# Turning the attention weights on VectorE with a DRAM bounce, in a two-layer trunk on one core

## The reference

```python
def memory_attention(q, mem_k, mem_v):            # 4 heads of 128, 256 memory tokens
    s = jnp.einsum('bthd,bmhd->bhtm', qh, kh) * (MEM_HEAD_DIM ** -0.5)
    p = jax.nn.softmax(s, axis=-1)
    o = jnp.einsum('bhtm,bmhd->bthd', p, vh)

def stick_breaking_attention(q, k, v):            # 12 heads of 128, causal
    mask = key_pos[None, :] < q_pos[:, None]
    z = jnp.einsum('bhqd,bhkd->bhqk', q_blk, kh) * scale
    log_beta = jax.nn.log_sigmoid(z)
    log_keep = jnp.where(mask, jax.nn.log_sigmoid(-z), 0.0)
    later = lax.cumsum(log_keep, axis=3, reverse=True) - log_keep
    w = jnp.where(mask, jnp.exp(log_beta + later), 0.0)
    o = jnp.einsum('bhqk,bhkd->bhqd', w, vh)
```

## Time and profile before

| | before |
|---|---|
| time, median of 3 runs | 1468.18 us |
| span of the profiled execution | 1466.5 us |
| TensorE busy | 1458.0 us, 99% |
| VectorE, ScalarE busy | 68%, 49% |
| chain that ended last | 99% TensorE |
| mean busy share of the DMA engines, 933 to 1248 us | about 0.8 |

### The profile page before, as it was taken

The page is one execution under the profiler, slowest core; times in us unless marked ns, Lnnn a source line. Parts: engine busy times, 40 slices in busy tenths (PEclk is TensorE's granted clock), DMA queues, the critical chain, the costliest instruction groups (busy, mean ns, idle before and its releaser), DMA issues.

```text
span 1466.5 us, 18207 instructions
## 1 busy us (share of the span) xinstructions
PE 1458.0 (99%) x6842; PEld 1221.7 (83%) x6842; DVE 997.5 (68%) x1317; ACT 716.3 (49%) x1066; POOL 122.8 (8%) x184
## 2 busy tenths in 40 slices
PE   9999999999999999999999999999999999999998
PEld 7888888888888888888888888888888888888886
DVE  6775568465576896856579676556566566578987
ACT  6764544444544645763325654433333433455465
POOL 0001111111110000000010001111111011000000
PEclk9999999999999999999999999999999999999999
DMA  9877788777886987477989876687888888858853
GB/s 344 290 287 225 159 215 228 174 235 158 212 251 165 323 323 260 155 262 282 358 326 372 291 224 219 244 218 196 230 241 244 202 239 208 226 188 329 315 200 144
DMA packets 154189, 357.97 MB, mean 244 GB/s; under 512 B 7824, under 2 KB 23440, under 8 KB 150032
## 3 DMA queue, kind: packets, MB, share of 16 engines
q1 hardware_dynamic: 103824, 205.98, 40.3%
q0 software_dynamic: 29376, 102.77, 28.3%
q10 hardware_dynamic: 20928, 48.41, 9.0%
HBM read 310.99 MB, written 113.25 MB: 289 GB/s over the span
## 4 chain that ended last, share of the span: by engine, by line
PE 99%; DMA 0%; SPq 0%; ACT 0%; issue 0%; DVE 0%; ACTq 0%
PE main L2128 25%; PE main L2127 25%; PE main L2126 25%; PE aux L2127 6%; PE aux L2126 6%; PE aux L2128 6%; PE aux L2484 2%; PE aux L2473 1%; DMA w_raw<-in_w_mem_kv 0%; PE aux L2270 0%; PE main L2178 0%; PE aux L2178 0%; PE main L2199 0%; PE main L2202 0%; PE main L2205 0%; PE aux L2220 0%
## 5 line engine op out<-in xcount | busy, mean ns | idle before, releaser
L2126 PE MATMUL main<-act_hi,w_hi 128*128 128x512 f32 x1216 | 475.3, 391 | 0.0
L2127 PE MATMUL main<-act_lo,w_hi 128*128 128x512 f32 x1216 | 473.6, 389 | 0.0
L2128 PE MATMUL main<-act_hi,w_lo 128*128 128x512 f32 x1216 | 473.6, 389 | 0.0
L2128 PEld LDWEIGHTS main<-act_hi,w_lo 128*128 128x128 f32 x1216 | 228.3, 188 | 47.4
L2127 PEld LDWEIGHTS main<-act_lo,w_hi 128*128 128x128 f32 x1216 | 228.4, 188 | 46.7
L2126 PEld LDWEIGHTS main<-act_hi,w_hi 128*128 128x128 f32 x1216 | 228.4, 188 | 46.4
L1334 DVE SCALAR_TENSOR_TENSOR w_lo<-w_raw,gains,w_hi 128x512 fp32r<-128x512 f32 x180 | 123.3, 746 | 120.5 <-ACT w_hi L704 120.5
L704 ACT ACTIVATE w_hi<-w_raw,gains 128x512 fp32r<-128x512 f32 x180 | 115.4, 712 | 140.6 <-PE main L2128 121.9
L1325 DVE TENSOR_TENSOR w_lo<-w_raw,w_hi 128x1024 fp32r<-128x1024 f32 x88 | 104.1, 1222 | 105.2 <-ACT w_hi L697 105.0
L697 ACT ACTIVATE w_hi<-w_raw 128x1024 fp32r<-128x1024 f32 x88 | 88.5, 1057 | 169.5 <-PE main L2128 132.7
L2126 PE MATMUL main<-w_hi,act_hi 128*128 128x512 f32 (+1 forms) x432 | 163.5, 378 | 0.0
(11 more groups left out here) (321 smaller groups left out, 1861.4 us busy)
## 6 DMA issues: line engine op xcount, KB each, us to landing
w_raw<-in_w_in_a SPq DMA_DIRECT2D x32, 1024.0 KB, 6.7
w_raw<-in_w_in_b SPq DMA_DIRECT2D x32, 1024.0 KB, 7.9
weight_sums<-in_w_out_a POOLq DMA_DIRECT2D x48, 512.0 KB, 7.0
weight_sums<-in_w_out_b POOLq DMA_DIRECT2D x48, 512.0 KB, 7.2
weight_sums<-weight_sums POOLq DMA_DIRECT2D x32, 512.0 KB, 6.4
w_raw<-weight_sums SPq DMA_DIRECT2D x16, 1024.0 KB, 6.6
work<-weight_sums SPq DMA_DIRECT2D x16, 1024.0 KB, 7.5
w_raw<-in_w_mem_kv SPq DMA_DIRECT2D x13, 1024.0 KB, 5.2
```

Of the source, the lines that this page charges most:

```text
L2126: TE.matmul(o, a[0], b[0], start=first, stop=False)
L2127: TE.matmul(o, a[0], b[1], start=False, stop=False)
L2128: return TE.matmul(o, a[1], b[0], start=False, stop=final)
```

## The change

TensorE's transposes are gone in both attentions. For each head, VectorE turns the weights in blocks of 32x32 (`V.transpose`) and lays them out so that a DMA can put the blocks of the four partition quarters in their places: ScalarE's queue stores 128 rows to DRAM (`turn_scratch`, 5 KB a row, or `prob_scratch`, 4 KB a row), waits for the store, and loads them back in four DMAs of 32 partitions, each row in four pieces of 1280 or 1024 bytes. The loads land in `wt_lo` or `pmt_lo`. ScalarE then copies the high part from there and VectorE subtracts in place. The values read the turned blocks with a strided pattern. The loads of keys and values move to SP's queue, between slab loads, each behind a wait for the values of the head two before. The heads' steps are laid out by slot; scores of head 1 are in slot 1, before head 0's values in slot 2, and so on. POOL's weight sums count on one semaphore, and each of the four groups waits for the group before.

```diff
@@ ScalarE @@
+            def turn_store(i, h):
+                act.wait_ge(wt_turned, 4 * (4 * i + h) + 4)
+                act.dma_start(turn_dram.rearrange("r i c m -> (r i) (c m)"), turned).then_inc(turn_stored, 16)
+
+            def turn_load(i, h):
+                n = 4 * i + h
+                act.wait_ge(turn_stored, 16 * (4 + n) + 16)
+                if h:
+                    act.wait_ge(o_done, n)
+                for c in range(4):
+                    act.dma_start(wt_lo[32 * c:32 * c + 32, :].rearrange("p (r m) -> p r m", r=4).bitcast(F32),
+                                  turn_dram[:, :, c, :].rearrange("r i m -> i r m")).then_inc(turn_loaded, 16)
+
+            def turned_high(i, h):
+                n = 4 * i + h
+                act.wait_ge(turn_loaded, 64 * (4 + n) + 64)
+                for b, w in enumerate(WT_WIDTH):
+                    part = slice(512 * b, 512 * b + w)
+                    nc.scalar.activation(wt_hi[:, part], wt_lo[:, part].bitcast(F32), ACT.Copy).then_inc(wt_high, 1)
...
                         split_next(G, j)
+                        if slot == 0:
+                            stick_weights(i, 0)
+                        if slot == 1:
+                            turn_store(i, 0)
+                            turn_load(i, 0)
+                            turned_high(i, 0)
+                            stick_weights(i, 1)
+                        if slot == 2:
+                            turn_store(i, 1)
+                            turn_load(i, 1)
+                        if slot == 3:
+                            turned_high(i, 1)
+                            stick_weights(i, 2)
+                        if slot == 4:
+                            turn_store(i, 2)
                             gate_sigmoid(2 * i + (G_B + 1))
+                            turn_load(i, 2)
+                            turned_high(i, 2)
+                        if slot == 5:
+                            stick_weights(i, 3)
+                            turn_store(i, 3)
+                        if slot == 6:
+                            turn_load(i, 3)
+                            turned_high(i, 3)
@@ ScalarE, memory head j @@
                         mem_head(L, j + 1)
+                    probs_store(L, j)
...
                     if j == 3:
                         act.wait_ge(sum_ready, 6 * L + 1)
                         y_quad(q_k1[0], 1)
+                    probs_load(L, j)
                 mem_probs_out(L, 3)
@@ VectorE, at the end of stick_weights @@
+                dve.wait_ge(w_ready, 4 * n + 4)
+                for k in range(NT):
+                    V.transpose(*turn_blocks(k)).then_inc(wt_turned, 1)
@@ VectorE, slots @@
+                        if slot == 5:
+                            turned_low(i, 2)
                         split_next(G, j)
...
                         if slot == 3:
+                            turned_low(i, 1)
                             dve.wait_ge(y_stored, 16 * i + 64)
                             dve.wait_ge(v_stored[3], 64)
                             gate_out(G, 0)
                             gate_out(G, 1)
+                            stick_weights(i, 2)
+                            gate_out(G, 2)
+                            gate_out(G, 3)
@@ VectorE, end of mem_norm_probs @@
+                dve.wait_ge(p_ready, 4 * L + n + 1)
+                V.transpose(pm_turned.rearrange("p (c n j) -> p n c j", c=4, j=32),
+                            pm.rearrange("p t (m c i) -> p (t m) c i", m=NMB, i=32)).then_inc(pt_turned, 1)
@@ SP @@
+            def load_kv(n):
+
+                if n > 1:
+                    sp.wait_ge(o_done, n - 1)
+                if n < 3:
+                    sp.wait_ge(v_stored[min(n + 1, 3)], 64)
+                sp.dma_start(kv[:, n % 2, :, :].bitcast(F32), kv_dram[n]).then_inc(kv_loaded[n % 2], 16)
@@ TensorE, hooks @@
+                        if slot == 0:
+                            hooks = {1: lambda: stick_scores(i, 0)}
+                        if slot == 1:
+                            hooks = {3: lambda: stick_scores(i, 1)}
+                        if slot == 2:
+                            hooks = {1: lambda: stick_values(i, 0)}
+                        if slot == 3:
+                            hooks = {2: lambda: stick_scores(i, 2), 3: lambda: stick_values(i, 1)}
+                        if slot == 5:
+                            hooks = {0: lambda: stick_scores(i, 3), 2: lambda: stick_values(i, 2)}
+                        if slot == 7:
+                            hooks = {0: lambda: stick_values(i, 3)}
@@ TensorE, memory attention and the projection behind it @@
-                    hooks = {(1 if j == 0 else 0): lambda: mem_scores(L, j), 3: lambda: mem_transposed(L, j)}
+                    hooks = {(1 if j == 0 else 0): lambda: mem_scores(L, j)}
...
-                half(s, 0, m01, 0, 0, values)
-                half(s, 1, m01, 0, 1)
+                half(s, 0, m01, 0, 0, freed(0))
+                half(s, 1, m01, 0, 1, values)
```

More of the change, by code:

```diff
@@ L63 @@
 WT_WIDTH = (512, 512, 256)
+TURN_AT = (0, 4, 7, 9)
+KV_LOADS = {8 * i + at: 4 * i + h for i in range(NPAIR) for at, h in ((7, 1), (10, 2), (11, 3), (13, 4))
+            if 4 * i + h < NB}
+PROB_TURN = (0, 16)
 Z_ORDER = ((1, 3, 0), (0, 2, 384), (2, 2, 0), (3, 1, 0))
@@ L222, in trunk, with probs_back @@
         pmt_lo = split_at("pmt_lo", [P, NMB, T], 2, 1024)
+        pm_turned = work[:, 1024:2048]
+        pmt_at = [w[:].rearrange("p m t -> p (m t)") for w in (pmt_hi, pmt_lo)]
+        def probs_back(w, m):
+            return w.rearrange("p (r t m j) -> p m t r j", r=4, t=NT, m=NMB)[:, m]
         mo = four(3)
@@ L430, in trunk @@
         q22_loaded = [sem(f"q22_loaded{n}") for n in range(2)]
-        sums_made = [sem(f"sums_made{n}") for n in range(4)]
+        sums_made = sem("sums_made")
         sum_ready = sem("sum_ready")
@@ L474, in load_in @@
                         sp.dma_start(x_nat[:, 2 + j, :], x_v[:, 2 + j, :]).then_inc(nat_loaded[1], 16)
+                if G0 == G_B:
+                    for q in range(1, 2 * NPAIR + 2):
+                        for j in range(4):
+                            n = KV_LOADS.get(4 * q + j)
+                            if n:
+                                load_kv(n)
+                            load_slab(G0 + q, j, w[:, in_column(q):in_column(q) + C])
+                    return
                 with sp.Fori(0, NPAIR - 1) as i:
@@ L2268, in mem_transposed @@
                 for m in range(NMB):
[L2269 to L2276 removed]
                     last = three_passes(aux[:, 2, :], (mv_hi[:, n % 2, m, :], mv_lo[:, n % 2, m, :]),
[L2278 removed]
+                                        [probs_back(w, m) for w in pmt_at], m == 0, m == NMB - 1)
                 last.then_inc(mo_done, 1)
@@ L2464, in stick_scores @@
                                  (kv[:, h % 2, 0, 0:w], kv[:, h % 2, 1, 0:w])).then_inc(z_done, 1)
-            def stick_transposed(i, h):
-                pe.wait_ge(w_ready, 4 * (4 * i + h) + 4)
-                for k in range(NT):
-                    bank, at = ((1, 0), (2, 0), (3, 0), (2, 384))[k]
-                    for t in range(k, NT):
-                        o = aux[:, bank, at + P * (t - k):at + P * (t - k) + P]
-                        c = T - P * (t + 1) + P * k
-                        last = TE.transpose(o, beta[:, t, c:c + P], ident[:])
-                last.then_inc(wt_done, 1)
             def stick_values(i, h):
```

216 lines of the change are left out of this document (112 added, 104 removed).

## The result

The changed kernel takes 1588.88 us (median of 4 runs, 1587.55 to 1589.55) against 1468.68 us of the kernel before on the same chip (4 runs, 1468.07 to 1469.37). The ratio is 1.0818, with a 95% interval of 1.0802 to 1.0833: 120 us slower. The forecast was 1492 us, its range ended at 1525. The sign and the mechanism were right; one term of the sum, the length of a trip in the loop, was 16.4 us where 11.0 stood, and the lower clock, which stood among the rivals, came on top.

The account below looks back on a forecast made before the run. TensorE was taken as the bound, busy 1458.0 of 1466.5 us. With the transposes' saving counted, the loop gave +9.9 and the memory attentions +14.4: +24.3 us, 1490.8 profiled, median 1492; 8-in-10 range 1447 to 1525.

Parts of the forecast that it names:

- The saving: TensorE's transposes removed: 13.1 us for 12 loop heads and 7.0 us for 8 memory heads, 20.1 us on the path.
- Turning on VectorE: VectorE's block transposes: 1.75 us for a loop head's four turns of 1280 columns; 1.2 us for a memory head.
- The chain, 66.2 + 4R: Loop turn length with four trips in sequence, R each; 110.2 us at R = 11.0, against 106.9 before.
- R in the loop: Loop trip, from last VectorE transpose to landing of the fourth load: 11.0 us, range 7.4 to 13.
- 5.5 a leg: Loop trip's store and its four loads, each put at 5.5 us by scaling the 7.2 us of 1 MB loads.
- the loop's term: Loop's part of the sum: a turn 3.3 us longer than before, three turns +9.9 us.
- Rival 3: Trips fall in step with GpSimd's bursts: trip 13 us in the loop, 11.8 in memory attentions; 1528 us, chance 0.12.
- 28.1 + 4R': Memory attention: time from slab 0's start to the last landing, four trips of R' each; +7.2 us per attention.
- R': Memory attention trip of 512 KB: 10.0 us for three heads, 8.5 for the last; break-even 7.8.
- Rival 4: TensorE's clock falls in gaps, a quarter slab at half speed after each of nine: 24 us more, 1516, chance 0.12.
- Key and value loads "hidden": Loop's key and value loads on SP's queue, with a slab load behind: wanted 22 us later against 8.5, so no cost.
- rivals 2 and 3: The first: in-between trips, 9.5 us in loop, 8.6 in memory attentions; 1465 us, chance 0.09. The second: see Rival 3.

Follow-up runs that it names:

- experiment 2: Changed kernel with each DMA of GpSimd's weight sums moving one row of 256 and the output projections reading input weights: 1507.1 us.
- experiment 3: Changed kernel with the loop's five trip DMAs moving an eighth of their bytes, high and low parts made from the turned blocks in place: 1544.6 us.
- experiment 4: Changed kernel with the loop's store cut into four DMAs of 1280-byte pieces and the load made one DMA: 1567.6 us.
- experiment 1: Changed kernel without both trips to DRAM, high and low parts made from the turned blocks in place: 1452.9 us, ratio 0.9893 to the kernel before.
- the filling: Changed kernel with matmuls without use in two gaps of each memory attention, loop untouched: 1582.4 us, ratio 1.0778 to the kernel before.
- experiment 5: Changed kernel with the loop's key and value loads moved from SP's queue to ScalarE's, behind the turned loads: 1590.5 us.

## Why the prediction was wrong, by its own steps

- **The saving**, 20.1 us, was right: without trips 1452.9, the turn 102.6.
- **Turning on VectorE**: 1024 columns take 1.25 us (1.2 put), four turns of a head 1.69 (1.75 put). Right.

```profile
426.64 1.25 DVE L1618 STREAM_TRANSPOSE work<-work 128x1024 f32<-128x1024 f32 x1
...
1051.65 1.69 DVE L2071 STREAM_TRANSPOSE work<-work 128x512 f32<-128x512 f32 x4
```

- **The chain, 66.2 + 4R**, was right in each of its parts. On ScalarE's and TensorE's timelines, second and third turn (us):

| part | forecast | experiment 2 | changed |
|---|---|---|---|
| values 3 to the next turn's first store | 28.2 | 28.3, 28.3 | 31.0, 30.3 |
| landing 0 to store 1 | 10.75 | 10.7 | 10.7 |
| landing 1 to store 2 | 12.0 | 11.9 | 11.9 |
| landing 2 to store 3 | 13.0 | 13.3 | 13.3 |
| landing 3 to values 3 | 2.25 | 2.4 | 2.4 |
| the turn's own four trips | 44.0 | 44.5, 43.9 | 61.9, 67.1 |

  What differs in the changed kernel besides the trips is the first line, the one in which the chain runs over TensorE's own work. That 131.8 came so near 131.2 has some luck in it: with the turn's own trips the formula gives 128.1 and 133.3, and the clock makes up the rest. Experiment 3's 120 us are 112 by the formula, 2.9 of clock, 3.9 of late keys and values, and 0.9 for the wait that its edit adds.
- **The step that failed is R in the loop.** "5.5 a leg": the store leg is that, 5.2. The load leg is 11.3, twice its term, and the ceiling of 13 for the trip lies at the least of the twelve. Three things were wrong in it. I scaled the 7.2 us of a 1 MB load down by its bytes, but experiment 3 shows that only a quarter of a trip goes with the bytes, and even those 7.2 became 11.1 with the trips beside them (median of the loop's ten). I took four DMAs as one with "three more issues"; the cut costs 1.7 to 3.5 us (experiment 4), and the issues are 0.31 to 2.16 us each. And I didn't ask what the new order issues beside the loads: SP's slab load behind VectorE's split (experiment 2). Twelve trips of 5.4 us more are 65 of the 73 us that the loop's term lacks; most of the rest is the clock, below.
- **Rival 3**, the step with GpSimd's bursts, was the right one, and too mild: it put the burst at 2 us a trip; experiment 2 shows 5.3. Its place is the load leg (11.3 to 8.1) more than the store's (5.2 to 3.0).
- **The memory attentions**: the second one bore out 28.1 + 4R'. Its trips are 11.5, 10.2, 9.6 and 7.5 us where I had 10, 10, 10 and 8.5; the last landing should come 66.9 us after slab 0's start and comes at 68.2. In the first the trips are 18.0, 14.0, 10.4 and 7.6: 78.0 by the formula, 79.1 measured. So R' was right for one stage and I gave it to both; in the first, GpSimd's sums are issued until 464.50, and with their bytes away (experiment 2) its trips are 12.3, 10.2, 9.4 and 7.6. These are the second stage's waits; the first values wait most, and the half slab behind the last values waits as well:

```profile
1381.27 0.77 PE L2245 MATMUL aux<-pmt_hi,mv_hi 128*128 128x512 f32 x1 [6.47 <-DVE pmt_lo L1625]
1398.22 0.48 PE L2245 MATMUL aux<-pmt_hi,mv_hi 128*128 128x512 f32 x1 [0.71 <-issue]
1425.56 0.47 PE L2245 MATMUL aux<-pmt_hi,mv_hi 128*128 128x512 f32 x1 [0.63 <-issue]
```

  They and the 3.46 us of the half slab are 11.3 us; I had put 10.7. Some 5 us I had not counted at all: with the same matmuls TensorE is busy 4.9 us longer than in experiment 1 from the first scores to the end (5.8 in the first memory attention's stretch), which is the lower clock.
- **Rival 4**, the clock: it does fall in the gaps, as the Trainium skill has it (TensorE: Matmul & The Clock Gate, Why this matters for your kernels). A turn of the changed kernel, in the columns of the row in experiment 1:

```profile
1073.09:1204.26 131.17, 109.99 (x480) 0.90 0.83 232
```

  TensorE is busy 110.0 us with work that takes 102.6 at full clock. Most of that costs nothing, since the chain of trips sets the turn and TensorE's waits are only shorter. But from values 3 to the next scores the chain runs over TensorE, and there the lower clock is paid. The changed kernel, then experiment 2, from values 3 to the next store:

```profile
1204.26 3.89 PE aux L2586 x12
...
1234.54 6.61 DMA turn_scratch<-work
```

```profile
1151.53 2.18 PE aux L2587 x12
...
1179.85 2.90 DMA turn_scratch<-work
```

  From values 3 to the next scores it is 18.3, 17.6 and 18.1 us against 15.7 each time: 6.9 us in the loop. With the 3 us that the filling gave back in the memory attentions, some 10 of the 37 us are shown on the path: less than the 24 of my rival, and not in my sum at all.
- **Key and value loads "hidden"**: not by name, 18.6 us of waits, for loads that take 14.4 us where I had 7.2. They hang behind values that are late themselves, and in the changed kernel each lands before the trip that VectorE waits for (experiment 5); with the shorter trips of experiment 3 one of them does cost.
- **Slips in the working.** 5.4 less 0.8 plus 1.2 is 5.8, not 5.6 (measured: 5.7 to 6.9 from a landing to the next store in the memory attentions). With 8.5 for the last trip the memory terms of rivals 2 and 3 are +3.0 and +12.6, not +2.5 and +13.3. None of them changes the outcome.

## What to carry to other kernels

The time of a small DMA beside heavy traffic is not its bytes' share of a large one's: count what it waits for, once for each DMA that must land, and take the issues with it. Look also at which loads the new order lets go at the same moment. Before a trip to DRAM replaces work on the busy engine, write down the chain with the trip as a letter; the formula with its break-even (here 10.2 us) was right when the number put into it was not, and it says what to try: not a shorter trip but one that runs beside the next step. And a clock that falls in a gap costs only where the engine is the one that the rest waits for; find that stretch on the chain and price it there.

## What the runs showed of the hardware

- GpSimd's transfers of 512 KB, which hold 42% of the DMA engines' time in the loop, add 5.3 us to a store and load pair of 640 KB on ScalarE's queue (11.1 to 16.4), and take the key and value loads of 1 MB from 8.3 to 11.1 us (medians of the loop's ten, experiment 2 and changed kernel).
- With GpSimd's bytes away, four loads of 160 KB take 4.7 to 4.9 us with no 1 MB load issued beside them at first, 7.6 to 8.9 with one issued within 1.0 us, and 10.7 to 11.2 with two just ahead and a third 6 us in.
- Five DMAs of 80 KB or 20 KB in this traffic take 12.3 us for the pair of store and loads, five of 640 and 160 KB 16.4.
- An issue on ScalarE's queue of a load of 32 partitions in four pieces takes 0.31 to 2.16 us, median 0.55; a store of 128 rows 0.35.
- 24 matmuls without use in a gap of about 12 us did not bring the mean granted clock of a turn above 0.92.
